# A 128-byte gap between the high and the low weight buffers of a three-product float32 block

## Chip, cores and metric

The kernel runs on one core of one Trainium2 chip. The metric is the device time of one execution in microseconds (us); smaller is better. The median of three runs of the kernel before is 1879.33 us.

## What is computed

One decoder block on 256 tokens with 16 learned tokens in front (272 in all), model width 2048, everything in float32. Two feed-forward blocks of width 5632 enclose a token mixer:

```python
def swiglu(h, w_gate, w_up, w_down):
    return (jax.nn.silu(h @ w_gate) * (h @ w_up)) @ w_down

hs = hs + 0.5 * swiglu(rmsnorm(hs, ffn1_norm), ffn1_w_gate, ffn1_w_up, ffn1_w_down)
hs = hs + token_mixing(rmsnorm(hs, mix_norm), w_in, ..., w_out)   # two causal convolutions
hs = hs + 0.5 * swiglu(rmsnorm(hs, ffn2_norm), ffn2_w_gate, ffn2_w_up, ffn2_w_down)
out = rmsnorm(hs, final_norm)[:, 16:]
```

The mixer projects to 5 x 1024 channels (w_in), convolves 1024 of them over 3 positions and 1024 over 31, and projects back (w_out). Nearly all work is in the matrix products.

## The kernel before, in words

**Three products for one.** A float32 product is made from three float32r products. Each weight block and each activation is split into a high part (a copy rounded to float32r) and a low part (what is left). The result is high x high + high x low + low x high. The helper product (L463 to L465) issues these three for one tile: w_high with act_high, w_high with act_low, w_low with act_high. Each matmul loads its own 128 x 128 weights ahead of it.

**The ring of weights.** All weights come from memory in 640 blocks of 512 KB: 128 partitions x 1024 floats, 4096 bytes a partition. SyncE loads a block into raw0 to raw3 in turn (load). ScalarE makes the high part, w_hi (high, L636). VectorE subtracts it from raw into w_lo (low, L859). TensorE waits for lo_ready, uses the block in 24 matmuls (16 or 12 in the last two stages) and raises block_used, which lets ScalarE write that buffer again. A column slice of 128 weights within a block is 512 bytes long, and slices begin at multiples of 512 bytes from the block's start.

**The stages**, in order, with the streamed columns of each matmul:

- gu1, the first up/gate product: 22 groups of 8 blocks, product on x_hi and x_lo, 272 columns
- down1: 4 groups of 22 blocks, product on a_hi and a_lo (the hidden activations, a1_hi and a1_lo in the code), 272 columns
- ag and cv: 4 groups of 8 blocks each, on x_hi and x_lo, 272 and 260 columns
- b: 2 groups of 8 blocks, on x_hi and x_lo, 256 columns
- out_sc and out_cf, the output projection in two parts: 4 groups of 4 blocks each, on y_hi and y_lo (y_both), 256 columns
- gu2: 22 groups of 8 blocks, wide_product (L470, L471): w_high with both parts of the activation at once (512 columns), then w_low with the high part (256 columns)
- down2: 4 groups of 22 blocks, last_group (L560 to L562): here the activations a_both are loaded as weights, and the weight block is what is streamed, 512 columns of w_hi, w_hi again and w_lo

Between blocks, VectorE and ScalarE also do the norms, the gates, the convolutions (conv_products, conv_adds) and what comes out of PSUM (finish).

**Where things lie.** Buffers are allocated one behind the other along each partition. A filler (to_512) brings x_region to a multiple of 512 bytes. From the sizes of the buffers follow the places, in bytes modulo 512:

- raw0 to raw3, w_hi0 to w_hi3, w_lo0 to w_lo3, then res, par, ident, ones and ident2: all 0
- x_hi: 0, and tile k, 272 floats or 1088 bytes long, at 64k; x_lo is 64 bytes further (X_GAP)
- a1_hi: 0, tile k at 64k; a1_lo at 448, that is 64 bytes before (A_GAP)
- y_both, x2_both and a2_both (the activations of out_sc, out_cf, gu2 and down2): 0 for both parts; their tiles are 256 floats or 1024 bytes long
- in cv the streamed columns begin 48 bytes into each tile, in b 64 bytes

The two helpers of the matmuls, and the loop around them in down2:

```python
pe.matmul(dst, w_high, act_high, start=first, stop=False)
pe.matmul(dst, w_high, act_low, start=False, stop=False)
return pe.matmul(dst, w_low, act_high, start=False, stop=last)
...
pe.matmul(wide, w_high, act_both, start=first, stop=False)
return pe.matmul(ps[:, bank, 0:SEQ], w_low, act_high, start=False, stop=last)
...
pe.matmul(dst, a_hi[:, k, toks], w_high, start=k == 0, stop=False)
pe.matmul(dst, a_lo[:, k, toks], w_high, start=False, stop=False)
m = pe.matmul(dst, a_hi[:, k, toks], w_low, start=False, stop=k == KF - 1)
```

Of the kernel before, what the change touches and what calls it, by code (L numbers as in the profile page):

```python
# [31 lines left out]
P = 128  # L32
# [7 lines left out]
def build(nc, x, meta_tokens, ffn1_norm, ffn1_w_gate, ffn1_w_up, ffn1_w_down, mix_norm, w_in, b_in,  # L40
# [40 lines left out]
    with ExitStack() as ctx:  # L81
        def sb(name, shape, dt=F32):
            return ctx.enter_context(nc.sbuf_tensor(name, shape, dt))
# [23 lines left out]

        raw = [sb(f"raw{i}", [P, BLOCK]) for i in range(RING)]
        w_hi = [sb(f"w_hi{i}", [P, BLOCK], F32R) for i in range(RING)]
        w_lo = [sb(f"w_lo{i}", [P, BLOCK], F32R) for i in range(RING)]  # L110
        res = sb("res", [P, KD, T])
        par = sb("par", [P, 4, P])
# [1097 lines left out]
```

## Time and profile before

| | |
|---|---|
| median of three runs | 1879.33 us (1879.24 to 1879.39) |
| the profiled execution | 1879.47 us |
| its span, first to last instruction | 1877.7 us |
| TensorE busy with matmuls | 1865.7 us, 13041 of them |
| VectorE busy | 1108.4 us |
| ScalarE busy | 919.0 us |
| moved by DMA | 342.26 MB, 182 GB/s |

Busy is the time in which an engine has at least one instruction under way. Matmuls overlap, so the mean duration of one is longer than the distance between two starts, and a count over a window includes those that began before it and had not ended. The clock row (PEclk) gives the TensorE clock granted, in tenths of full speed, in 40 slices of the span.

### The profile page before, as it was taken

The numbers are of one execution on the slowest core, as the hardware profiler recorded it, in microseconds if no ns is written. First come the engines' busy times: TensorE is split into PE (matmuls) and PEld (weight loads), VectorE is DVE, ScalarE is ACT, GpSimd is POOL, SyncE is SP. The second block draws the span as 40 slices with busy tenths as digits, with TensorE's granted clock in tenths as the row PEclk, the third lists the DMA queues.
The fourth block names the chain that finished last, engine by engine and source line by source line (L and its number), as shares of the span: only waits on it lengthen the run. The fifth ranks groups of instructions, "written<-read, shape, count | busy, mean of one in ns | idle before, by whom it ended". The sixth has DMA issues, their size and how long they took to land.

```text
span 1877.7 us, 32134 instructions
## 1 busy us (share of the span) xinstructions
PE 1865.7 (99%) x13041; PEld 1761.3 (94%) x13041; DVE 1108.4 (59%) x1212; ACT 919.0 (49%) x1167; POOL 5.9 (0%) x17
## 2 busy tenths in 40 slices
PE   9999999999999999999999999999999999999998
PEld 9999999999999999999999998888888888888886
DVE  7555555555554454468899887555666555544444
ACT  6433434334433344369888565444444444433343
POOL 1000000000000000000000000000000000000000
PEclk9999999999999999999999999999999999999999
DMA  6655555555555555555666566666656666666664
GB/s 222 193 175 178 170 177 177 171 177 176 171 179 174 174 177 172 178 170 173 187 186 182 167 196 188 190 188 188 185 179 192 192 196 190 213 188 185 193 186 134
DMA packets 283357, 342.26 MB, mean 182 GB/s; under 512 B 10639, under 2 KB 223985, under 8 KB 283152
## 3 DMA queue, kind: packets, MB, share of 16 engines
q1 hardware_dynamic: 282672, 340.44, 58.5%
q8 instruction: 57, 0.93, 0.2%
q10 hardware_dynamic: 320, 0.53, 0.1%
q0 software_dynamic: 288, 0.19, 0.0%
q14 instruction: 20, 0.16, 0.0%
HBM read 339.02 MB, written 2.10 MB: 182 GB/s over the span
## 4 chain that ended last, share of the span: by engine, by line
PE 98%; DVE 1%; DMA 0%; ACT 0%; SPq 0%; issue 0%; DVEq 0%
PE ps L464 20%; PE ps L463 20%; PE ps L465 20%; PE ps L470 17%; PE ps L471 9%; PE ps L560 4%; PE ps L562 4%; PE ps L561 4%; PE ps L577 0%; DMA x_tok<-in_x 0%; DVE w_lo L859 0%; PE ps L425 0%; DVE zc L1060 0%; DVE ln_mu L885 0%; SPq L320 0%; PE ps L485 0%
## 5 line engine op out<-in xcount | busy, mean ns | idle before, releaser
L859 DVE TENSOR_TENSOR w_lo<-raw,w_hi 128x1024 fp32r<-128x1024 f32 x639 | 781.5, 1224 | 662.1 <-ACT w_hi L636 656.9
L636 ACT ACTIVATE w_hi<-raw 128x1024 fp32r<-128x1024 f32 x639 | 675.5, 1058 | 853.9 <-PE ps L465 513.6
L463 PE MATMUL ps<-x_hi,w_hi 128*128 128x272 f32 (+2 forms) x2048 | 588.1, 287 | 1.2 <-DVE x_lo L868 1.2
L464 PE MATMUL ps<-x_lo,w_hi 128*128 128x272 f32 (+2 forms) x2048 | 587.2, 287 | 0.0
L465 PE MATMUL ps<-x_hi,w_lo 128*128 128x272 f32 (+2 forms) x2048 | 583.4, 285 | 0.0
L470 PE MATMUL ps<-x_both,w_hi 128*128 128x512 f32 x1408 | 488.6, 394 | 0.0
L471 PE MATMUL ps<-x_both,w_lo 128*128 128x256 f32 x1408 | 390.1, 277 | 0.0
L464 PEld LDWEIGHTS ps<-x_lo,w_hi 128*128 128x128 f32 x2048 | 386.4, 189 | 0.1
L463 PEld LDWEIGHTS ps<-x_hi,w_hi 128*128 128x128 f32 x2048 | 384.6, 188 | 1.5 <-DVE w_lo L1082 1.4
L465 PEld LDWEIGHTS ps<-x_hi,w_lo 128*128 128x128 f32 x2048 | 385.4, 188 | 0.0
L470 PEld LDWEIGHTS ps<-x_both,w_hi 128*128 128x128 f32 x1408 | 264.0, 188 | 61.3
L471 PEld LDWEIGHTS ps<-x_both,w_lo 128*128 128x128 f32 x1408 | 264.4, 188 | 0.0
L465 PE MATMUL ps<-a_hi,w_lo 128*128 128x272 f32 x704 | 203.1, 289 | 0.0
L463 PE MATMUL ps<-a_hi,w_hi 128*128 128x272 f32 x704 | 202.4, 288 | 0.0
L464 PE MATMUL ps<-a_lo,w_hi 128*128 128x272 f32 x704 | 202.4, 287 | 0.0
L560 PE MATMUL ps<-w_hi,a_both 128*128 128x512 f32 x352 | 137.3, 390 | 0.0
L562 PE MATMUL ps<-w_lo,a_both 128*128 128x512 f32 x352 | 137.0, 389 | 0.0
L561 PE MATMUL ps<-w_hi,a_both 128*128 128x512 f32 x352 | 136.9, 389 | 0.0
L463 PEld LDWEIGHTS ps<-a_hi,w_hi 128*128 128x128 f32 x704 | 132.9, 189 | 0.0
L464 PEld LDWEIGHTS ps<-a_lo,w_hi 128*128 128x128 f32 x704 | 132.3, 188 | 0.0
L465 PEld LDWEIGHTS ps<-a_hi,w_lo 128*128 128x128 f32 x704 | 132.3, 188 | 0.0
L738 ACT ACTIVATE tap_product<-z,par 128x256 f32<-128x256 f32 x232 | 98.8, 495 | 0.0
(141 smaller groups left out, 1150.3 us busy)
## 6 DMA issues: line engine op xcount, KB each, us to landing
raw<-in_ffn_w_up SPq DMA_DIRECT2D x176, 512.0 KB, 3.6
raw<-in_ffn_w_down SPq DMA_DIRECT2D x176, 512.0 KB, 4.6
raw<-in_ffn_w_gate SPq DMA_DIRECT2D x175, 512.0 KB, 3.8
raw<-in_w_in SPq DMA_DIRECT2D x80, 512.0 KB, 3.5
raw<-in_w_out SPq DMA_DIRECT2D x32, 512.0 KB, 4.6
x_tok<-in_x SPq DMA_DIRECT2D x4, 512.0 KB, 7.8
gain_tok<-in_final_norm SPq DMA_DIRECT2D x1, 1024.0 KB, 7.0
out_y<-o_tok SPq DMA_DIRECT2D x2, 512.0 KB, 2.8
```

Source lines behind the costliest of these rows:

```text
L463: pe.matmul(dst, w_high, act_high, start=first, stop=False)
L464: pe.matmul(dst, w_high, act_low, start=False, stop=False)
L465: return pe.matmul(dst, w_low, act_high, start=False, stop=last)
L470: pe.matmul(wide, w_high, act_both, start=first, stop=False)
L471: return pe.matmul(ps[:, bank, 0:SEQ], w_low, act_high, start=False, stop=last)
L560: pe.matmul(dst, a_hi[:, k, toks], w_high, start=k == 0, stop=False)
L561: pe.matmul(dst, a_lo[:, k, toks], w_high, start=False, stop=False)
L562: m = pe.matmul(dst, a_hi[:, k, toks], w_low, start=False, stop=k == KF - 1)
L636: act.activation(w_hi[s][:, :], raw[s][:, :], ACT.Copy).then_inc(hi_ready, 1)
L738: act.activation(tap_product[:, q % PRODUCTS, c % 2, :], z[:, c, 2 + n:2 + n + SEQ], ACT.Copy, scale=cf_tap(2 + n, c)).then_inc(cf_product, 1)
L859: dve.tensor_tensor(w_lo[s][:, :], raw[s][:, :], w_hi[s][:, :].bitcast(F32), ALU.subtract).then_inc(lo_ready, 1)
```

## The change

One tensor of 128 bytes a partition, which nothing reads or writes, is allocated between the high and the low weight buffers. Everything allocated behind it begins 128 bytes later: w_lo0 to w_lo3, res, par, ident, ones and ident2. The instructions and their order are the same on every engine. The lines of the code behind it have numbers one higher.

```diff
         raw = [sb(f"raw{i}", [P, BLOCK]) for i in range(RING)]
         w_hi = [sb(f"w_hi{i}", [P, BLOCK], F32R) for i in range(RING)]
+        sb("lo_by", [P, 32])
         w_lo = [sb(f"w_lo{i}", [P, BLOCK], F32R) for i in range(RING)]
         res = sb("res", [P, KD, T])
         par = sb("par", [P, 4, P])
```

## Rows read from the trace of the kernel before

**Rows 1.** The page: TensorE's busy time, and its granted clock in 40 slices.
```profile
PE 1865.7 (99%) x13041; PEld 1761.3 (94%) x13041; DVE 1108.4 (59%) x1212; ACT 919.0 (49%) x1167; POOL 5.9 (0%) x17
...
PEclk9999999999999999999999999999999999999999
```

**Rows 2.** The page: the chain that ended last, by engine.
```profile
PE 98%; DVE 1%; DMA 0%; ACT 0%; SPq 0%; issue 0%; DVEq 0%
```

**Rows 3.** Waits of TensorE: us in total, times, longest us.
```profile
PE ps L425 <- DMA x_tok<-in_x: 1.3, 1, 1.3
...
PE ps L463 <- DVE w_lo L859: 0.5, 1, 0.5
```

**Rows 4.** Windows in down1, cv and b: us, TensorE busy (matmuls), clock, DMA.
```profile
600.00:800.00 200.00, 200.00 (x1597) 1.00 0.57 175
...
910.00:980.00 70.00, 70.00 (x591) 1.00 0.60 183
1000.00:1035.00 35.00, 35.00 (x299) 1.00 0.64 192
```

**Rows 5.** Timeline of TensorE in gu1: start us, us, engine, line, operation.
```profile
200.14 0.28 PE L465 MATMUL ps<-x_hi,w_lo 128*128 128x272 f32 x1
200.26 0.29 PE L463 MATMUL ps<-x_hi,w_hi 128*128 128x272 f32 x1
200.38 0.29 PE L464 MATMUL ps<-x_lo,w_hi 128*128 128x272 f32 x1
200.51 0.29 PE L465 MATMUL ps<-x_hi,w_lo 128*128 128x272 f32 x1
...
201.64 0.28 PE L465 MATMUL ps<-x_hi,w_lo 128*128 128x272 f32 x1
```

**Rows 6.** The same in out_cf; eight matmuls are left out between.
```profile
1099.79 0.28 PE L465 MATMUL ps<-y_both,w_lo 128*128 128x256 f32 x1
...
1100.87 0.28 PE L465 MATMUL ps<-y_both,w_lo 128*128 128x256 f32 x1
```

**Rows 7.** Timeline of all engines in gu2; two pairs of matmuls.
```profile
1300.12 0.40 PE L470 MATMUL ps<-x_both,w_hi 128*128 128x512 f32 x1
1300.12 0.19 PEld L471 LDWEIGHTS ps<-x_both,w_lo 128*128 128x128 f32 x1
...
1300.47 0.39 PE L470 MATMUL ps<-x_both,w_hi 128*128 128x512 f32 x1
...
1300.81 0.40 PE L470 MATMUL ps<-x_both,w_hi 128*128 128x512 f32 x1
```

**Rows 8.** Timeline of TensorE in down2; two matmuls are left out between.
```profile
1699.97 0.39 PE L562 MATMUL ps<-w_lo,a_both 128*128 128x512 f32 x1
...
1700.65 0.39 PE L562 MATMUL ps<-w_lo,a_both 128*128 128x512 f32 x1
```

**Rows 9.** Matmuls with w_lo: count, ns min/median/max, first and last start us.
```profile
L465 PE MATMUL ps<-x_hi,w_lo x2048: 277/283/295, 10.7 to 1040.1; 128*128 128x272 f32 x152, 128*128 128x260 f32 x23, 128*128 128x256 f32 x12
...
L471 PE MATMUL ps<-x_both,w_lo x1408: 274/280/284, 1134.3 to 1622.8; 128*128 128x256 f32 x176
...
L465 PE MATMUL ps<-a_hi,w_lo x704: 284/288/296, 542.5 to 807.0; 128*128 128x272 f32 x176
...
L562 PE MATMUL ps<-w_lo,a_both x352: 388/389/395, 1623.3 to 1869.3; 128*128 128x512 f32 x176
...
L465 PE MATMUL ps<-y_both,w_lo x256: 278/283/287, 1040.5 to 1134.0; 128*128 128x256 f32 x128
```

**Rows 10.** Groups by line and form: busy us, mean ns, idle before and releasers.
```profile
L859 DVE TENSOR_TENSOR w_lo<-raw,w_hi 128x1024 fp32r<-128x1024 f32 x639 | 781.5, 1224 | 662.1 <-ACT w_hi L636 656.9
L636 ACT ACTIVATE w_hi<-raw 128x1024 fp32r<-128x1024 f32 x639 | 675.5, 1058 | 853.9 <-PE ps L465 513.6 <-PE ps L471 195.7 <-PE ps L562 136.6
L910 DVE TENSOR_TENSOR t<-ps,gu_lo 128x1024 f32<-128x1024 f32 x22 | 26.9, 1224 | 53.2 <-ACT gu_lo L669 53.1
```

## The prediction

> **What bounds the kernel now.** I read the page's busy times first. [rows 1] TensorE is busy for 1865.7 of 1877.7 us, at a granted clock of full speed (the 2.4 GHz level) from the first slice to the last. The chain that ended last is TensorE for 98% and VectorE for 1% [rows 2]. The longest wait of a matmul anywhere is 1.3 us, and for the low weights in a ring buffer TensorE waited once, 0.5 us [rows 3]. So the time is the number of matmuls times their pitch (the time from one start to the next), plus a dozen us at the ends. Only a change of the pitch can move this kernel.
>
> So the pitch is to be taken apart. A matmul is listed as 0.27 to 0.40 us long, but the next one starts long before it ends, so only the distance of starts counts. In the output projection (256 columns) nine starts take 1.08 us from 1099.79 to 1100.87: 120.0 ns each [rows 6]. In the last stage (512 columns) three take 0.68 us: 226.7 ns [rows 8]. The 256 columns more cost 106.7 ns, 0.417 ns a column, one column per cycle at 2.4 GHz. That leaves a **fixed part** of 120.0 - 106.7 = 13.3 ns in either. In the second up/gate stage a 512-column and a 256-column matmul alternate: two pairs take 1300.81 - 1300.12 = 0.69 us [rows 7], 0.347 us a pair, and 0.347 - 0.320 = 0.027 us is again 13.3 ns a matmul. In the first up/gate stage (272 columns, 113.3 ns) twelve take 1.50 us [rows 5]: 125.0 ns, a fixed part of 11.7 ns. For three more stages the windows give the pitch; each count holds about two matmuls that began earlier, so I take two off [rows 4]. The first down projection gives 200/1595 = 125.4 ns (12.1 over its columns), the stage with 260 columns 70/589 = 118.8 ns (10.5 over), the one with 256 columns on the normalised x 35/297 = 117.8 ns (11.2 over).
>
> The **addresses** explain a part of this. Every weight buffer begins at 0 modulo 512, and a slice of 128 weights is 512 bytes, so each weight load now begins at 0. The activations differ by stage. In the output projection, the second up/gate stage and the last stage a tile of activations is 1024 bytes and high and low lie multiples of 512 apart: everything is at 0, and the fixed part is 13.3 ns in all three. In the other stages tile k is 1088 bytes, so it begins at 64k modulo 512, the low part 64 bytes further (or, for the first down projection, 64 bytes before), and the fixed part is 10.5 to 12.1 ns. At equal width the two cases are 120.0 and 117.8 ns. So where operands lie is worth about 2 ns a matmul. What the trace doesn't tell is whether it is the place of the activation by itself or its place relative to the weights. A warning that position modulo 512 is not all: in the second up/gate stage two successive pairs take 0.35 and 0.34 us [rows 7] although they are alike modulo 512.
>
> **The change, part by part.** No instruction is added, removed or reordered on any engine; the weights of a block need no byte more. w_lo0 to w_lo3 begin at 128 modulo 512, and so do res, par, ident, ones and ident2 behind them.
>
> Term 1, loads of low weights. A weight load starts with the matmul ahead of it (1300.12 for both in [rows 7]) and so reads beside that matmul's activations. Where all is at 0 it now begins 128 bytes off. These are 256 loads in the output projection and 1408 in the second up/gate stage [rows 9]. Term 2, the last stage, in which the low weights are the streamed operand: 352 matmuls [rows 9]. Together 2016 matmuls. No row shows such an operand 128 bytes off alone. The bounds: at best the whole fixed part goes, 2016 x 13.3 ns = 26.8 us; at worst each takes what the dearest single pitch shown adds to the mean (0.35 us against 0.347 for a pair [rows 7], 3 ns), 6 us. The nearest row is the stage of equal width with shifted activations, 117.8 against 120.0: 2.2 ns, times 2016 = 4.4 us less. That is the price if the relative place counts. If the place of the activation alone counts, term 1 is 0 and term 2 at most 352 x 2.2 ns = 0.8 us less.
>
> Term 3, the stages with 1088-byte tiles: 2048 + 704 = 2752 loads of low weights [rows 9]. Here tile k already stands at 64k to the weights and runs through all eight places. A shift of the low weights by 128, two of these steps, exchanges the places among the k and leaves their mean. I take 0. If the mean moves all the same, the bounds are the cheapest and the dearest fixed part of rows: from 11.7 to 10.5 ns, 2752 x 1.2 = 3.3 us less, and from 11.7 to 13.3, 2752 x 1.6 = 4.4 us more.
>
> Term 4, ScalarE and VectorE. The subtraction that writes w_lo takes 1224 ns, and a subtraction of the same size with PSUM and another tile as sources takes 1224 ns too [rows 10], so its time shows nothing of where operands lie; I take 0. VectorE is idle for 656.9 us waiting for the high part, and ScalarE for over 800 us waiting for TensorE to free a buffer [rows 10]: they cover some 1 us a block. Without that cover, at the start and around 1073 to 1085 us, where the chain passes through VectorE for 1% of the span [rows 2], 5% on its operations would be under 1 us. The shifted res, par and identities are read by these engines and by a few dozen transposes and adds: nothing.
>
> The sum. Whether the relative place counts is about even. Without it the sum is -0.8 to 0 us; with it -4.4 us, and term 3 blurs that by several us either way. The single likeliest outcome is that no difference can be told: the profiled execution took 1879.47 us, the median shown is 1879.33, so I forecast 1879.3 us. A measurement of this kernel can tell some 0.2% from no change, that is 3.8 us.
>
> A rule against any effect: rows show 120.0 and 117.8 ns at equal width with the operands placed differently, so some of the pitch depends on place [rows 4, 6]. The Trainium skill, "TensorE: Matmul & The Clock Gate", section "Step-by-step: what each phase is for", says TensorE has two independent read ports and that loading the next weights doesn't take bandwidth from the running matmul; by that rule terms 1 to 3 are all 0 and the sum is the time of before, while by the rows term 1 and 2 may be -4.4 us. The trace doesn't bear it out fully, since a fixed part that varies from 10.5 to 13.3 ns has no place in it.
>
> **The rivals.**
> 1. Faster: the relative place counts. For it: 13.3 ns in all three stages in which everything is at 0, whatever the width and whichever operand is streamed, and less everywhere else. Against it: in those other stages the activations were shifted, not the weights, and in each only a third to a half of the loads would change now. Price: 2.2 ns x 2016 = 4.4 us, 1874.9 us; with the cheapest fixed part shown (10.5) it is 2.8 x 2016 = 5.6 us, 1873.7 us, and 3.3 us more of term 3 gives 1870.4 us.
> 2. Slower: the low part of the activations lies 64 bytes from the high part beside high and low weights at the same place. If what keeps the stages on x and on the first hidden activations at 11.7 ns is this combination, not each place by itself, then with w_lo 128 bytes off they go to the 13.3 ns of the other stages. On the 2752 matmuls beside the low loads alone: 4.4 us, 1883.7 us; on all 8256 of these stages: 13.2 us, 1892.5 us. It decides from a pitch of 125.5 instead of 125.0 ns in the first up/gate stage. For it: inside a product the pitches of three matmuls are unequal there (starts 0.12 and 0.13 us apart [rows 5]), so they depend on more than one operand. Against it: the first down projection, with its low part on the other side, comes out within 0.4 ns.
> 3. The shift isn't there: an allocator that rounded w_lo0 up to 512 bytes would shift nothing modulo 512, and the time is 1879.3 us. Tiles of 32 bytes stand packed elsewhere in this program, so I give it almost nothing; it is counted in the forecast.
>
> **How the numbers follow.** The forecast, with rival 3 in it: 0.43. Rival 1: 0.33. Rival 2: 0.24. The likeliest case's own range is 1876 to 1882. The range that should hold the time 8 times in 10 takes in rival 1 with its cheapest fixed part and part of what could come on top, and rival 2 on the low loads with a part of the rest: 1869 to 1886 us. The chances of faster, same and slower by 0.2% are those of the three cases, 0.33, 0.43, 0.24; rival 1 lies just beyond the bound at 4.4 us, and I leave it there, since a single low operand off the common place may also save more than the mean over eight places.
>
> **What would show it.** Right: the pitch of every stage stays within 0.3 ns (1.50 us for twelve, 1.08 for nine, 0.69 for two pairs, 0.68 for three), w_lo stays at 1224 ns. Rival 1: the second up/gate stage, 488.5 us now from the first to the last of its 1408 low matmuls [rows 9], gets shorter by over 3 us, and the output projection goes under 120.0 ns. Rival 2: the first up/gate stage needs over 1.505 us for twelve. The forecast is wrong if any stage's pitch moves by over 1 ns, or if a wait for w_lo appears beside the one of 0.5 us.

## The result, and the profile after

The changed kernel takes 1894.41 us (median of 4 runs, 1894.33 to 1894.56) against 1879.29 us before: 15.1 us more, a ratio of 1.008 (95% interval 1.0068 to 1.0092). The forecast of no change was wrong, and the time lies outside the range that I gave.

What changed on the page against [rows 1, 2] is TensorE's time. It is busy for 1881.1 us, 15.4 more, in a span of 1892.8 us, and its weight loads (PEld) for 11.8 us more. The clock row and the chain are the same, and VectorE's and ScalarE's sums are so within 0.1 us.

```profile
PE 1881.1 (99%) x13041; PEld 1773.1 (94%) x13041; DVE 1108.3 (59%) x1212; ACT 918.9 (49%) x1167; POOL 5.9 (0%) x17
...
PEclk9999999999999999999999999999999999999999
...
PE 98%; DVE 1%; DMA 0%; ACT 0%; SPq 0%; issue 0%; DVEq 0%
```

TensorE's waits, the view of [rows 3], are what they were, but for 0.3 us less at the very start (1.0 us for x_tok, before 1.3). So no wait came in, and the whole loss is in the pitch, the distance from one start to the next:

```profile
PE ps L464 <- DVE x_lo L869: 1.2, 1, 1.2
...
PE ps L426 <- DMA x_tok<-in_x: 1.0, 1, 1.0
PE ps L464 <- DVE w_lo L860: 0.5, 1, 0.5
```

Where it went is read from the first and last starts of the matmuls that use w_lo, the view of [rows 9] (count, ns, first and last start in us):

```profile
L466 PE MATMUL ps<-x_hi,w_lo x2048: 277/288/297, 10.7 to 1049.0; 128*128 128x272 f32 x152, 128*128 128x260 f32 x23, 128*128 128x256 f32 x12
L472 PE MATMUL ps<-x_both,w_lo x1408: 274/281/281, 1142.7 to 1631.0; 128*128 128x256 f32 x176
L466 PE MATMUL ps<-a_hi,w_lo x704: 284/288/292, 549.2 to 814.0; 128*128 128x272 f32 x176
L563 PE MATMUL ps<-w_lo,a_both x352: 395/395/398, 1631.6 to 1884.4; 128*128 128x512 f32 x176
L466 PE MATMUL ps<-y_both,w_lo x256: 274/281/288, 1049.4 to 1142.3; 128*128 128x256 f32 x128
```

down1 begins at 549.2 instead of 542.5 us, so gu1 alone lost 6.7 us. gu2 takes 488.3 us from its first to its last low matmul (before 488.5). down2 takes 252.8 us (before 246.0). Two stages hold 13.6 of the 15.1 us. The windows of [rows 4], laid over four stages of the kernel after (us, TensorE busy and matmuls, clock), tell the same:

```profile
100.00:300.00 200.00, 200.00 (x1581) 1.00 0.56 173
...
600.00:800.00 200.00, 200.00 (x1595) 1.00 0.57 174
...
1150.00:1350.00 200.00, 200.00 (x1155) 1.00 0.61 187
1650.00:1850.00 200.00, 200.00 (x884) 1.00 0.59 183
```

In gu1 this is 200/1579 = 126.7 ns a matmul, where twelve starts gave 125.0 before. In down2 three starts span 0.70 us, by the timeline below, where [rows 8] had 0.68:

```profile
1699.84 0.40 PE L563 MATMUL ps<-w_lo,a_both 128*128 128x512 f32 x1
1700.08 0.39 PE L561 MATMUL ps<-w_hi,a_both 128*128 128x512 f32 x1
1700.31 0.40 PE L562 MATMUL ps<-w_hi,a_both 128*128 128x512 f32 x1
1700.54 0.40 PE L563 MATMUL ps<-w_lo,a_both 128*128 128x512 f32 x1
```

Not only the matmul on the low weights grew. Over the whole stage the medians of the distances from each of the three to the next one's start (in the order high x high, high x low, low x high) are 230, 236 and 234 ns; before they were 226, 227 and 227.

The timeline of gu1 shows how the loss is spread there. Four products are twelve matmuls:

```profile
300.02 0.28 PE L464 MATMUL ps<-x_hi,w_hi 128*128 128x272 f32 x1
...
300.39 0.29 PE L464 MATMUL ps<-x_hi,w_hi 128*128 128x272 f32 x1
...
300.77 0.29 PE L464 MATMUL ps<-x_hi,w_hi 128*128 128x272 f32 x1
...
301.15 0.29 PE L464 MATMUL ps<-x_hi,w_hi 128*128 128x272 f32 x1
...
301.54 0.28 PE L464 MATMUL ps<-x_hi,w_hi 128*128 128x272 f32 x1
```

The distances are 0.37, 0.38, 0.38 and 0.39 us, 1.52 in all against 1.50 before. With the starts averaged over the stage, the four products take 371, 378, 376 and 395 ns; before they took 373, 377, 373 and 377. The same four numbers return, within 1 ns, through all groups but the first and the first four products of the second. TensorE runs in a repeating pattern: a fixed cycle of unequal distances.

### The profile page after: what moved, and what is told of

Its sections match the earlier page's. It is cut to its first block, busy times and chain, and to the rows that moved or that the text cites. A ratio compares the mean times of both kernels' runs of the same rounds, so it can differ in the third digit from the quotient of the medians.

```text
span 1892.8 us, 32134 instructions
## 1 busy us (share of the span) xinstructions
PE 1881.1 (99%) x13041; PEld 1773.1 (94%) x13041; DVE 1108.3 (59%) x1212; ACT 918.9 (49%) x1167; POOL 5.9 (0%) x17
## 4 chain that ended last, share of the span: by engine, by line
PE 98%; DVE 1%; DMA 0%; ACT 0%; SPq 0%; issue 0%; DVEq 0%
PE ps L466 20%; PE ps L465 20%; PE ps L464 19%; PE ps L471 17%; PE ps L472 9%; PE ps L562 4%; PE ps L563 4%; PE ps L561 4%; PE ps L578 0%; DMA x_tok<-in_x 0%; DVE w_lo L860 0%; PE ps L426 0%; DVE zc L1061 0%; DVE ln_mu L886 0%; SPq L321 0%; PE ps L486 0%
## 5 line engine op out<-in xcount | busy, mean ns | idle before, releaser
L860 DVE TENSOR_TENSOR w_lo<-raw,w_hi 128x1024 fp32r<-128x1024 f32 x639 | 781.4, 1224 | 676.6 <-ACT w_hi L637 671.9
L466 PE MATMUL ps<-x_hi,w_lo 128*128 128x272 f32 (+2 forms) x2048 | 590.8, 288 | 0.0
L471 PE MATMUL ps<-x_both,w_hi 128*128 128x512 f32 x1408 | 488.5, 392 | 0.0
L472 PE MATMUL ps<-x_both,w_lo 128*128 128x256 f32 x1408 | 395.6, 281 | 0.0
L562 PE MATMUL ps<-w_hi,a_both 128*128 128x512 f32 x352 | 139.9, 397 | 0.0
L561 PE MATMUL ps<-w_hi,a_both 128*128 128x512 f32 x352 | 138.4, 393 | 0.0
```

The lines of the kernel that those rows point to most:

```text
L860: dve.tensor_tensor(w_lo[s][:, :], raw[s][:, :], w_hi[s][:, :].bitcast(F32), ALU.subtract).then_inc(lo_ready, 1)
```

## The experiments

The table gives the stages of the runs that only move buffers (the last version comes further below). Each time is in us, from the start of the stage's first matmul to the start of the next stage's first (for down2, to the start of its own last). The first line is the kernel before, the others are differences from it, all computed from the starts of the matmuls in the traces. Each experiment, but the last version, is a single execution. Still, what runs have in common repeats well: the stages of the change and of the run with w_lo allocated last agree within 0.03 us up to out_cf and in down2, and gu2's +9.17 and +6.04 each came twice. A filler also moves whatever is allocated behind it, the tile of ones included; this matters for gu2 alone, as will be seen.

| run | gu1 | down1 | ag | cv | b | out_sc | out_cf | gu2 | down2 |
|---|---|---|---|---|---|---|---|---|---|
| before | 531.84 | 264.88 | 96.46 | 91.33 | 45.28 | 47.81 | 46.08 | 488.76 | 246.44 |
| the change (w_lo +128) | +6.74 | +0.30 | +1.25 | +0.84 | -0.10 | -0.25 | -0.34 | -0.12 | +6.87 |
| rest only +128 | 0.00 | 0.00 | +0.01 | 0.00 | 0.00 | 0.00 | 0.00 | +9.17 | 0.00 |
| w_hi and w_lo +128 | +0.08 | +0.14 | 0.00 | +0.01 | +0.01 | -0.37 | -0.51 | +6.04 | +5.83 |
| w_lo +128, allocated last | +6.75 | +0.29 | +1.25 | +0.84 | -0.10 | -0.25 | -0.34 | +4.46 | +6.84 |
| everything +128 | 0.00 | 0.00 | 0.00 | 0.00 | 0.00 | 0.00 | 0.00 | 0.00 | 0.00 |
| weights and a2_both +128 | +0.08 | +0.14 | 0.00 | +0.01 | +0.01 | -0.36 | -0.51 | +6.04 | +0.01 |
| w_lo +256 | -0.01 | 0.00 | 0.00 | 0.00 | 0.00 | +0.01 | 0.00 | 0.00 | 0.00 |
| only ones +128 | +0.01 | 0.00 | +0.01 | 0.00 | 0.00 | 0.00 | 0.00 | +9.17 | 0.00 |
| w_lo +64 | +4.64 | -0.88 | +0.84 | +0.80 | -0.11 | -0.60 | -0.85 | -0.21 | +5.43 |
| w_lo +192 | -2.12 | +2.30 | -0.39 | +0.83 | 0.00 | -0.62 | -0.85 | -0.12 | +2.20 |

**Is it the low weights, or what moved with them?** The filler behind w_lo instead of ahead of it moves only res, par and the identities and ones:

```diff
         w_lo = [sb(f"w_lo{i}", [P, BLOCK], F32R) for i in range(RING)]
+        sb("res_by", [P, 32])
         res = sb("res", [P, KD, T])
```

> The 128 bytes stand behind the low weights instead of ahead of them: high and low weights are at 0 modulo 512 as before, and only res, par and the identities lie 128 bytes later. Theory A (the time is lost by the place of w_lo against other operands of TensorE): every stage as before, 1879.3 us, first up/gate stage 531.7 us, last stage 246.4 us. Theory B (it is the place of res, par or the identities, read and written by VectorE and ScalarE): 1894 us as with the change.

Measured: 1888.42 us. Neither theory held. Eight stages are as before to 0.01 us, as theory A has it, and yet 9.2 us are lost, all of them in gu2, which with the whole change had lost nothing. Its 1408 low matmuls begin over 497.5 us here, where [rows 9] have 488.5:

```profile
L472 PE MATMUL ps<-x_both,w_lo x1408: 277/281/284, 1134.2 to 1631.7; 128*128 128x256 f32 x176
```

The counterpart allocates w_lo last, with the filler ahead of it. Everything else keeps its place modulo 512:

```diff
-        w_lo = [sb(f"w_lo{i}", [P, BLOCK], F32R) for i in range(RING)]
...
         ident2 = sb("ident2", [P, P])
+        sb("lo_by", [P, 32])
+        w_lo = [sb(f"w_lo{i}", [P, BLOCK], F32R) for i in range(RING)]
```

> The low weights at 128 modulo 512 as in the change, but allocated last, so that res, par and the identities are at 0 as before. The run with these alone shifted lost 9.2 us, all of it in the second up/gate stage. Theory A (low weights against the other operands of TensorE cost the first up/gate, ag and cv stages and the last stage): these stages as with the change, +6.7, +1.3, +0.8 and +6.9 us. The second up/gate stage: if it is in one of a few repeating patterns that a disturbance at its start picks, any of 346.7 or 353.3 ns a pair may come, nothing between. Theory B (res, par and identities cause the loss): all stages as before.

Measured: 1899.12 us. The seven stages up to out_cf and down2 repeat the change's losses to 0.03 us: they come from the low weights alone. gu2 comes out in yet another way, +4.46 us, 350 ns a pair (the 512-column matmul and the 256-column one behind it). "346.7 or 353.3, nothing between" was wrong: there are more patterns than two. It also shows that the change left gu2 unharmed by luck: the low weights alone cost it 4.5 us, the things behind them alone 9.2 us, and both together, as in the change, nothing.

**Which distance counts?**

```diff
         raw = [sb(f"raw{i}", [P, BLOCK]) for i in range(RING)]
+        sb("hi_by", [P, 32])
         w_hi = [sb(f"w_hi{i}", [P, BLOCK], F32R) for i in range(RING)]
```

> The filler stands ahead of the high weights: high and low weights both at 128 modulo 512, the activations where they were. Theory A1 (what counts is that high and low weights differ from each other): as before, 1879.3 us, the last stage at 226.7 ns a matmul. Theory A2 (what counts is the place of weights against activations): not as before. In the last stage all three matmuls stream weights that lie 128 bytes off their loaded activations, so that it should lose at least the 6.9 us that it lost with the low weights alone, up to three times that, 1886 to 1900 us.

Measured: 1890.64 us. Each of the two theories holds in some stages. gu1, ag and cv are as before within 0.08 us, and down1 begins at 542.6 us as in [rows 9]: there it is the distance of high from low weights that cost 8.8 us.

```profile
L466 PE MATMUL ps<-a_hi,w_lo x704: 284/287/296, 542.6 to 807.2; 128*128 128x272 f32 x176
```

But down2 lost 5.83 us, though high and low are at the same place: there the distance of the streamed weights from the loaded activations counts. The lower bound that I gave for it, 6.9 us, was too high, so the losses of three shifted matmuls don't add.

The next run keeps this and moves the activations of down2 by the same 128 bytes (and gu2_lo behind them, which TensorE doesn't read):

```diff
-        a2_both = at("a2_both", a_at, [P, 2, KF, SEQ], F32R)
+        a2_both = at("a2_both", a_at + 128, [P, 2, KF, SEQ], F32R)
```

> High and low weights at 128 as in the run with both shifted (last stage +5.8 us), and now the activations of the last stage are at 128 too. If the last stage loses by the distance between its streamed weights and its loaded activations, it is back at 246.4 us and everything else is as in that run (first up/gate +0.1). If it loses by the absolute place of the weights, it stays at 252.3 us.

Measured: 1884.77 us, and down2 is back. The view of the matmuls with w_lo, of the run with the weights alone and then of this run:

```profile
L563 PE MATMUL ps<-w_lo,a_both x352: 388/393/404, 1628.7 to 1880.5; 128*128 128x512 f32 x176
```

```profile
L563 PE MATMUL ps<-w_lo,a_both x352: 388/389/398, 1628.6 to 1874.6; 128*128 128x512 f32 x176
```

251.8 us became 246.0, the time of before, by the place of the loaded operand.

One filler ahead of all buffers moves everything by 128 bytes:

```diff
+        sb("all_by", [P, 32])
         x_at = nc.sbuf_base
```

> One filler of 128 bytes ahead of all activations and weights: everything moves together. If only relative places count, every stage keeps its time to 0.1 us, with the second up/gate stage as the only one that might fall into its other pattern (+9.2 us). If absolute places modulo 512 count, the stages whose operands all were at 0 (output projection, second up/gate, last) change and the last stage is not at 246.4 us.

Measured: 1879.54 us, every stage as before. For TensorE's operands only distances count.

**What is the period?** The filler between high and low weights is 64 floats wide:

```diff
-        sb("lo_by", [P, 32])
+        sb("lo_by", [P, 64])
```

> A gap of 256 bytes in place of 128. In the trace of before the first up/gate stage repeats with every fourth tile k, that is every 256 bytes. If places count modulo 256, all stages are as before, last stage 246.4, first up/gate stage 531.8 us (second up/gate stage in either pattern). If they count modulo 512, 256 bytes are the farthest place and the last stage and first up/gate stage lose again, by 3 us or more each.

Measured: 1879.4 us, every stage as before to 0.01 us. A gap of 256 bytes is no gap. The 512 that I reckoned with is twice the period. The next two runs have fillers of 16 and of 48 floats, 64 and 192 bytes.

> Low weights 64 bytes after the place of the high ones. If only distances modulo 256 count, each stage gets a time of its own. By the size of the loss with 128 bytes I expect a loss in the last stage between 0 and 6.9 us and in the first up/gate stage between 0 and 6.7 us; a rival is that 128, half the period, was the mildest place and 64 loses more.

Measured: 1888.42 us. Both losses lie in the ranges expected, +4.64 and +5.43 us. down1 gained 0.88 us and the output projection 1.45.

> 192 bytes, that is 64 bytes ahead of the high weights modulo 256, if 256 is the period. Streams that run upward have no reason to be symmetric in the sign of the distance, so I expect times that differ from those with 64 by over 1 us in the first up/gate or the last stage; equal times would mean that only the size of the distance counts.

Measured: 1880.69 us. The sign of the distance matters: gu1 gains 2.1 us where 64 bytes lost 4.6, and down1 turns the other way. Both places off 0 speed up the output projection by 1.5 us. In both runs ones moved along; the last version below has it at its old place and repeats, within 0.05 us, the values for 192 bytes in gu1, the output projection and gu2, and that for 64 in down1.

**Why did gu2 move by itself?** Of the tensors moved in the first run TensorE reads one within gu2: ones, loaded once as weights for the sums of squares in the middle of the first group.

```diff
-        ones = sb("ones", [P, P])
         ident2 = sb("ident2", [P, P])
+        sb("ones_by", [P, 32])
+        ones = sb("ones", [P, P])
```

> Only the tile of ones lies 128 bytes later; all else is as before. In the first group of the second up/gate stage TensorE loads it once as weights, for the sums of squares (one matmul among 2816). Theory P (a lone matmul disturbs a repeating pattern, and where its weights lie decides which pattern follows): the second up/gate stage takes 9.2 us longer, all others as before, 1888.4 us. Theory Q (the place of res acts, through VectorE's and ScalarE's reads): as before, 1879.3 us.

Measured: 1888.55 us, gu2 +9.17 us and nothing else: theory P. The timeline at that matmul (L485 before, L486 here; start us, us), first of the kernel before:

```profile
1144.00 0.40 PE L470 MATMUL ps<-x_both,w_hi 128*128 128x512 f32 x1
...
1145.06 0.40 PE L470 MATMUL ps<-x_both,w_hi 128*128 128x512 f32 x1
...
1145.42 0.59 PE L485 MATMUL ps<-sq_sum,ones 128*128 128x256 f32 x2
1145.67 0.58 PE L470 MATMUL ps<-x_both,w_hi 128*128 128x512 f32 x1
...
1146.20 0.40 PE L470 MATMUL ps<-x_both,w_hi 128*128 128x512 f32 x1
...
1146.55 0.39 PE L470 MATMUL ps<-x_both,w_hi 128*128 128x512 f32 x1
...
1146.89 0.40 PE L470 MATMUL ps<-x_both,w_hi 128*128 128x512 f32 x1
```

and of this run, at the same place and 153 us later:

```profile
1145.33 0.59 PE L486 MATMUL ps<-sq_sum,ones 128*128 128x256 f32 x2
1145.57 0.59 PE L471 MATMUL ps<-x_both,w_hi 128*128 128x512 f32 x1
...
1146.11 0.40 PE L471 MATMUL ps<-x_both,w_hi 128*128 128x512 f32 x1
...
1299.45 0.40 PE L471 MATMUL ps<-x_both,w_hi 128*128 128x512 f32 x1
...
1299.81 0.40 PE L471 MATMUL ps<-x_both,w_hi 128*128 128x512 f32 x1
...
1300.16 0.40 PE L471 MATMUL ps<-x_both,w_hi 128*128 128x512 f32 x1
...
1300.51 0.40 PE L471 MATMUL ps<-x_both,w_hi 128*128 128x512 f32 x1
```

The first pair after the sums takes 0.53 us in the one and 0.54 in the other, some 10 ns apart. From there on the kernel before takes 343 and 350 ns in turn for a pair, and this run 350, 361 and 349, three pairs in 1.06 us. It stays so for the 21 groups that follow, in which no wait of TensorE is listed: 6.6 ns a pair times 1376 pairs is 9.1 us.

The two lines ahead of the sums say more. Three pairs span 1144.00 to 1145.06 us, 1.06 us, in the kernel before too: over nearly the whole half group ahead of the sums it cycles through 350, 361 and 349 ns, like this run. So the slow pattern is the one in which gu2 begins in both. With ones at 0 the sums throw TensorE out of it into the fast one, and with ones at 128 they don't.

If a lone matmul can pick the pattern, a matmul in each group should pick it anew. So a kick, one more matmul whose result is overwritten, goes ahead of every group of gu2 but the first, 64 columns wide ahead of the even groups and 128 ahead of the odd ones. The addresses are those of before:

```diff
+                    if phase == "gu2" and not first_group:
+                        pe.matmul(ps[:, SET * parity, 0:64 + 64 * parity], ones[:, :], ones[:, 0:64 + 64 * parity],
+                                  start=True, stop=True)
                     for i in range(n_blocks[phase]):
```

> Addresses as before; each group of the second up/gate stage but the first begins with one more matmul of ones, 64 or 128 columns wide in turn, into a bank that is then overwritten. Its own cost is its columns plus the fixed part, 40 and 67 ns. Theory P: groups take 22.2 or 22.6 us (346.7 or 353.3 ns a pair), or the other sums seen with shifted weights, and change between them from group to group. Theory R (the pattern is set by the addresses of the stage alone): every group 22.2 us plus the kick, 490 us in all.

Measured: 1888.53 us. Groups take 22.83 and 22.41 us in turn, with the wide and the narrow kick. Windows inside three successive groups (us, TensorE busy and matmuls, clock) and two pieces of the timeline:

```profile
1204.00:1224.00 20.00, 20.00 (x115) 1.00 0.60 186
1226.00:1246.00 20.00, 20.00 (x118) 1.00 0.62 188
1249.00:1269.00 20.00, 20.00 (x115) 1.00 0.62 185
```

```profile
1189.08 0.40 PE L470 MATMUL ps<-x_both,w_hi 128*128 128x512 f32 x1
...
1190.12 0.39 PE L470 MATMUL ps<-x_both,w_hi 128*128 128x512 f32 x1
...
1212.02 0.40 PE L470 MATMUL ps<-x_both,w_hi 128*128 128x512 f32 x1
...
1213.08 0.40 PE L470 MATMUL ps<-x_both,w_hi 128*128 128x512 f32 x1
```

Three pairs take 1.04 us after a narrow kick and 1.06 after a wide one (the first two lines and the last two), with the same instructions on operands at the same places modulo 256. Theory P holds, theory R is out. The width isn't the only difference between the kicks: the wide one always goes with the odd groups, which use the other four banks of PSUM. The groups of before alternate between the same banks at 22.19 us each, but whether width or bank makes the kicks differ was not separated. A narrow kick itself costs 0.22 us (22.41 less 22.19), not the 40 ns that I expected: the product of two plain float32 tiles stands in the trace as two matmuls, as for the sums above (x2).

The same test on gu1, in the changed kernel:

```diff
+                        if phase == "gu1" and not first_group and i == 0:
+                            pe.matmul(ps[:, SET * parity, 0:64 + 64 * parity], ones[:, :], ones[:, 0:64 + 64 * parity],
+                                      start=True, stop=True)
```

> The changed kernel (low weights at 128), with one more matmul of ones, 64 or 128 columns wide in turn, in each group of the first up/gate stage but the first, ahead of the group's first product. Question: is the slow pattern of that stage (four products of 395, 371, 378 and 376 ns, 126.7 ns a matmul against 125.0) forced by the addresses, or one of several that a disturbance picks, as in the second up/gate stage? Forced: all groups fall back into it, the stage is at 538.5 us plus 21 kicks of 0.1 to 0.2 us, 541 to 543 us. One of several: some groups take 24.0 us or another sum, and kinds of groups alternate with the kick's width.

Measured: gu1 at 543.1 us, 4.5 more than with the change alone, and 21 x 0.22 = 4.6 is the price of the kicks. Every group, after either kick, is back at 395, 371, 378 and 376 ns after four products (within 1 ns). Inside a group four products take 1.52 us, as without kicks:

```profile
299.74 0.29 PE L464 MATMUL ps<-x_hi,w_hi 128*128 128x272 f32 x1
...
301.26 0.29 PE L464 MATMUL ps<-x_hi,w_hi 128*128 128x272 f32 x1
```

With the low weights at 128 this pattern was the only one that two kinds of kick could reach.

**A version that beats both.** The low buffers get a distance for each stage:

```diff
+        lo_at = nc.sbuf_base + 256
+        sb("lo_region", [P, RING * BLOCK + 112])
+        LO_SHIFT = {'gu1': 192, 'down1': 64, 'ag': 0, 'cv': 0, 'b': 0,
+                    'out_sc': -64, 'out_cf': -64, 'gu2': -64, 'down2': -256}
...
+        w_lo = {phase: [at(f"w_lo_{phase}{i}", lo_at + by + 4 * BLOCK * i, [P, BLOCK], F32R) for i in range(RING)]
+                for phase, by in LO_SHIFT.items()}
```

The distances only fall from stage to stage, so that a block of a new stage never reaches into a later buffer that still holds a block of the old one.

> A version that should beat both kernels: the low weights get a distance for each stage, from the runs with 64 and 192 bytes: 192 in the first up/gate stage, 64 in the first down projection, 0 in ag, cv and b, 192 in the output projection and the second up/gate stage, 0 in the last. The low buffers are allocated last, so ones, res and the rest stay at 0. If the stages are independent of each other, the differences measured add: -2.1, -0.9, -1.5, -0.1 us, in all -4.6 us, 1874.8 us. If the second up/gate stage falls into a slower pattern because it is entered in another state, up to 9.2 us come back, 1884 us at most.

Measured: 1874.79 us (median of 11) against 1879.43, a ratio of 0.998 (interval 0.9971 to 0.9989). The stages give -2.07, -0.89, -0.62, -0.85 and -0.12 us, and 0.00 for the others: -4.56 in all, the sum expected. In the trace down1 ends 3.1 us and gu2 begins 4.5 us sooner than in [rows 9]:

```profile
L469 PE MATMUL ps<-a_hi,w_lo_down x704: 284/287/292, 540.3 to 803.9; 128*128 128x272 f32 x176
...
L475 PE MATMUL ps<-x_both,w_lo_gu x1408: 274/278/285, 1129.8 to 1618.1; 128*128 128x256 f32 x176
```

Two of the 11 executions took 1879.6 and 1879.7 us, the time of before, so the gain doesn't come every time. A stage that fell into another pattern would look like this, but the profiled execution was not one of them, so that stays open.

## Why the prediction was wrong

**What held.** TensorE's pitch is the whole time, no wait appeared, and term 4 was right: the subtraction still takes 1224 ns, and VectorE's and ScalarE's sums are within 0.1 us. The pitch does depend on distances between operands. That everything at one place is the dearest case did not hold.

**Term 3** failed first and most. I let the activations run through all places against the low weights and concluded that a shift "exchanges the places among the k and leaves their mean. I take 0". Measured: +6.74, +1.25, +0.84, +0.30 and -0.10 us, 9.0 in all, above the bound of 4.4. The step looked only at the distance between the low weights and the activations, which runs through all places. The run with both weights shifted shows that the distance between high and low weights is another one, which does not run through anything: with it at 0 again, the loss is gone. Rival 2 named this combination, high and low weights at the same place beside the two parts of the activations. In gu1 its level is met as well: four products in 395 + 371 + 378 + 376 = 1520 ns are 126.7 ns a matmul, a fixed part of 13.3 ns, and ag is the same. Its decision point, 125.5 ns, was passed. In down1, with 2112 matmuls, the same level would have cost over 2 us and 0.30 came; b lost nothing. So its whole-product price of 13.2 us, which the range left out, was too high, and its price on the low loads alone, 4.4 us, too low.

**Term 2** had its sign wrong. I priced the 352 low matmuls of down2 at 2.2 ns less each, 0.8 us, and bounded a loss by 3 ns on each of them, 1.1 us. Measured: 6.87 us more, because all 1056 matmuls of the stage, not the 352 alone, went from 226.7 to about 233.3 ns on average. The premise was that everything at 0 is the worst place because it showed 13.3 ns. In down2 it is the best of the four places tried (64: +5.43, 128: +6.87, 192: +2.20 us). From three stages at the same place there was nothing to learn about other places.

**Term 1** was sized as 2.2 ns on 1664 matmuls, 3.7 us less. The output projection gained 0.59 us and gu2 0.12. Even this 0.12 isn't the worth of the low weights' place: with ones left where it was, the same shift cost gu2 4.46 us. With gaps of 0, 64, 128 and 192 bytes gu2 can rest at 346.7 ns a pair, but at 128 it did so only with ones shifted too. The terms measured, 9.0 and 6.9 us more and 0.7 less, make up the loss (15.2 us by the stages of the trace, 15.1 by the medians).

**The hint that I passed over.** I noted that two successive pairs in gu2 took 0.35 and 0.34 us though they were alike modulo 512, and wrote only that position "is not all". This alternation was the mark of a pattern in time: each matmul's pitch depends on the ones before it, so a sum of prices per matmul could not carry the case. A look at gu2's first half group would have shown 1.06 us for three pairs in place of 1.04 (three times 346.7 ns), in the same stage on the same addresses. The rule that the Trainium skill gives in "TensorE: Matmul & The Clock Gate", section "Step-by-step: what each phase is for" (the next weights' load takes no bandwidth from the running matmul), was read in the prediction as a rule against any effect of place; so read, it would make all runs with the same instructions equal. They differ by up to 24 us (1874.8 to 1899.1), and down2 by the distance between what it loads and what it streams, so the measurements decide against that reading here.

**What stays open.** Why a given distance is dear, and what within TensorE's reads keeps the patterns alive, no run shows. Nor does any show what in the sums' matmul decides which pattern gu2 goes on in, or how gu2's time depends on the distance of weights from activations: the run with both weights shifted, +6.04 us there, moved ones as well. High weights alone at 128 were not tried: with a filler on either side of them, bringing the rest back to its place takes 512 bytes, and 480 are free.

## What to carry to other kernels

When TensorE never waits, measure the pitch by stage and look at it product by product: a cycle of unequal times (343 and 350, or 350, 361 and 349 ns) means that the stage sits in a pattern, and then a lone matmul in it can be worth 2% of the stage, as in gu2. Place operands by trying the distances modulo 256 (0, 64, 128 and 192 between high weights, low weights and activations), stage by stage, since the best distance of one stage can be the worst of another (192 bytes here, for gu1 and down1); here the gains of separate stages added. Compare layouts by the stages' own times: a filler that moved only one operand of gu2, read once, cost 9.2 us in gu2, which by the total alone would be blamed on the wrong tensor. And run a layout several times: the last version gave its gain in 9 of 11 executions.

## What the runs showed that I had not expected

- Places counted modulo 256 bytes and only as distances: a gap of 256 between the weights, or 128 ahead of everything, changes no stage by more than 0.01 us.
- One loop on one set of addresses has at least two steady speeds: 346.7 and 353.3 ns a pair in gu2. The kernel before shows both, the slow one until the sums in its first group and the fast one after. One matmul's place (128 bytes) or form (a kick of 64 or 128 columns, each with its own banks) chose between them. Shifted weights gave 350 and 351 ns too.
- In gu1, with the low weights at 128, only one was found: it returns to its pattern within four products after either kick.
- A low operand 128 bytes off slows the matmuls that don't use it as well: in down2 two of three read the same bytes as before, and the three distances grew by 4, 9 and 7 ns (2 to 4%).
